# Two transformer blocks on one core: the differential attention's scores in three fp32r passes over high and low parts

## The reference

```python
def diff_attend(q, k, v, lam):
    s = jnp.einsum('bqhmd,bkhmd->bhmqk', q, k).astype(jnp.float32) * (DIFF_QK ** -0.5)
    p = jax.nn.softmax(s, axis=-1)
    a = p[:, :, 0] - lam * p[:, :, 1]
    return jnp.einsum('bhqk,bkhd->bqhd', a.astype(v.dtype), v)
...
    q = apply_rope_2d(group(z, G_DQ).reshape(B, N, HEADS, 2, DIFF_QK), ang_r, ang_c)
    k = apply_rope_2d(group(z, G_DK).reshape(B, N, HEADS, 2, DIFF_QK), ang_r, ang_c)
    v = group(z, G_DV).reshape(B, N, HEADS, HEAD_DIM_2)
    k_all = jnp.concatenate([kc, k], axis=1)
    v_all = jnp.concatenate([vc, v], axis=1)
```

## Time and profile before

| | |
|---|---|
| median of 3 runs | 3357.74 us (3357.29 to 3358.83) |
| the profiled execution | 3358.63 us, span 3357.3 us |
| TensorE busy | 3243.3 us (97%) |
| VectorE busy | 2150.5 us (64%) |
| ScalarE busy | 1389.9 us (41%) |
| mean granted TensorE clock | 0.991 |
| layer 2's attention loop | 1968 to 2113 us |
| layer 3's attention loop | 2814 to 2924 us |

### The profile page before, as it was taken

How to read it: one execution, slowest core, us unless ns; L and a number is a source line. 1 busy time by engine, 2 the same in 40 slices (tenths; PEclk the granted TensorE clock), 3 DMA queues, 4 the chain that set the end, 5 groups by cost and what they waited for, 6 DMA issues and landing times. The chain is left out here.

```text
span 3357.3 us, 45065 instructions
## 1 busy us (share of the span) xinstructions
PE 3243.3 (97%) x17830; PEld 2767.6 (82%) x17830; DVE 2150.5 (64%) x3560; ACT 1389.9 (41%) x2242; POOL 221.0 (7%) x336
## 2 busy tenths in 40 slices
PE   7998999999999999999999999999999999999998
PEld 5787789999978888878878886889999987688887
DVE  5678477888665545558788466476777865654444
ACT  5478353333444324342223345353333444542332
POOL 0001100000000000003111000100000010010001
PEclk9999999999999999999999999999999999999999
DMA  6500124444221221226664211113333231122232
GB/s 242 201 23 1 38 74 128 144 132 140 91 93 46 101 78 47 88 76 200 204 200 167 85 45 51 38 67 116 113 104 110 83 103 57 44 88 94 94 101 76
DMA packets 98689, 334.39 MB, mean 100 GB/s; under 512 B 11872, under 2 KB 16768, under 8 KB 95024
## 3 DMA queue, kind: packets, MB, share of 16 engines
q1 hardware_dynamic: 77072, 252.63, 22.4%
q0 software_dynamic: 21408, 78.88, 7.4%
HBM read 329.37 MB, written 2.10 MB: 99 GB/s over the span
## 5 line engine op out<-in xcount | busy, mean ns | idle before, releaser
L1245 ACT ACTIVATE WH<-WR 128x1024 fp32r<-128x1024 f32 (+3 forms) x516 | 443.1, 863 | 916.0 <-PE PS L638 679.5
L1862 DVE TENSOR_TENSOR WL<-WR,WH 128x1024 fp32r<-128x1024 f32 (+3 forms) x516 | 507.9, 986 | 449.1 <-ACT WH L1245 447.9
L638 PE MATMUL PS<-HH,WH 128*128 128x512 f32 x1608 | 544.2, 373 | 8.7 <-DVE WK L2295 3.4
L638 PE MATMUL PS<-HH,WL 128*128 128x512 f32 x1608 | 539.7, 370 | 0.0
L638 PE MATMUL PS<-HL,WH 128*128 128x512 f32 x1608 | 539.2, 369 | 0.0
L638 PE MATMUL PS<-D,WH 128*128 128x512 f32 x1648 | 420.9, 361 | 1.5 <-DVE D L2319 1.4
L638 PEld LDWEIGHTS PS<-HH,WH 128*128 128x128 f32 x1608 | 280.6, 189 | 69.6 <-issue 9.9
L638 PEld LDWEIGHTS PS<-HL,WH 128*128 128x128 f32 x1608 | 279.4, 189 | 52.8 <-issue 1.0
L638 PEld LDWEIGHTS PS<-HH,WL 128*128 128x128 f32 x1608 | 279.7, 189 | 52.2
L638 PEld LDWEIGHTS PS<-D,WH 128*128 128x128 f32 x1648 | 275.7, 188 | 52.6 <-DVE D L2319 3.2
L638 PE MATMUL PS<-D,WL 128*128 128x512 f32 (+1 forms) x824 | 257.3, 360 | 0.0
(11 more groups left out here) (377 smaller groups left out, 6042.5 us busy)
## 6 DMA issues: line engine op xcount, KB each, us to landing
WR<-in_win SPq DMA_DIRECT2D x176, 512.0 KB, 3.5
AT<-in_adat POOLq DMA_DIRECT2D x144, 512.0 KB, 3.9
WR<-in_wret SPq DMA_DIRECT2D x64, 512.0 KB, 3.7
WR<-in_zin SPq DMA_DIRECT2D x36, 512.0 KB, 3.5
WR<-in_wdn SPq DMA_DIRECT2D x32, 448.0 KB, 3.4
WR<-in_wdn SPq DMA_DIRECT2D x48, 256.0 KB, 2.7
WR<-in_wdn SPq DMA_DIRECT2D x32, 320.0 KB, 3.0
AR<-in_ada SPq DMA_DIRECT2D x8, 1024.0 KB, 19.1
```

The costliest lines, as they stand in the source:

```text
L638: mm = PE.matmul(dst[:, a:b], w(u)[:, k * P:(k + 1) * P], h[:, k, a:b], start=(k == 0 and i == 0), stop=(k == nk - 1 and i == 2))
L1245: AC.activation(M.hi(u), M.raw(u), COPY).then_inc(*on.up("w_hi", u))
L1862: VE.tensor_tensor(M.lo(u), M.raw(u), M.hi(u).bitcast(F32), ALU.subtract).then_inc(*on.up("w_lo", u))
```

## The change

The rotated queries and keys get fp32r copies: QH and KH, the high parts, written by ScalarE in four new copies (`score_high`), and QL and KL, the low parts, written by VectorE in four subtractions at the place of Z's slots 10 and 11 and of DK themselves. ScalarE's four stand around its refills u + 4 + ROWS_AT and u + 5 + ROWS_AT, VectorE's four behind its refill u + 5 + ROWS_AT. The first score waits for the last subtraction, where it waited for the last rotation. Each score is the sum of three matmuls in fp32r (QH x KH, QL x KH, QH x KL), with the two maps' matmuls alternating and the strips as before. The tile NIL shrinks from 768 columns to one that is read broadcast, and CN0, a table of the Fourier mixer, moves behind the new tiles.

```diff
@@ class Memory, mixers @@
+        at = Z + 10 * 4 * T
         self.DK = t("DK", [P, 2, T])
...
-        self.NIL = t("NIL", [P, T])
-        self.top = Z + 96 * 1024
+        self.NIL = t("NIL", [P, 1])
+        self.QH = t("QH", [P, 2, T], F32R)
+        self.KH = t("KH", [P, 2, T], F32R)
         self.CN = [t("CN0", [P, 2, S])]
+        self.top = at
+        self.QL = t("QL", [P, 2, T], F32R)
+        self.KL = t("KL", [P, 2, T], F32R)
@@ tensor_program, mixers @@
                 if j == 0:
-                    PE.wait_ge(*on("roped", (l, 3)))
+                    PE.wait_ge(*on("roped", (l, "low", 3)))
                 w, c0 = nm * P, m0 * P
                 rows = [slice(64 * (h % 2) + 32 * mp, 64 * (h % 2) + 32 * mp + 32) for mp in range(2)]
                 for a in range(0, w, 512):
                     e = min(w, a + 512)
-                    for mp, r in enumerate(rows):
-                        if j and a == 0:
-                            PE.wait_ge(*on("d_max", (l, j - 1, mp)))
-                        mm = PE.matmul(PS[mp][:, a:e], M.Z[r, 10 + h // 2, q * P:(q + 1) * P], M.DK[r, h // 2, c0 + a:c0 + e],
-                                       start=True, stop=True, tile_position=(r.start, 0))
-                        if e == w:
-                            mm.then_inc(*on.up("d_scores", (l, j, mp)))
+                    for i, (qs, ks) in enumerate(((M.QH, M.KH), (M.QL, M.KH), (M.QH, M.KL))):
+                        for mp, r in enumerate(rows):
+                            if j and a == 0 and i == 0:
+                                PE.wait_ge(*on("d_max", (l, j - 1, mp)))
+                            mm = PE.matmul(PS[mp][:, a:e], qs[r, h // 2, q * P:(q + 1) * P], ks[r, h // 2, c0 + a:c0 + e],
+                                           start=i == 0, stop=i == 2, tile_position=(r.start, 0))
+                            if e == w and i == 2:
+                                mm.then_inc(*on.up("d_scores", (l, j, mp)))
@@ scalar_program, mixers @@
-        for v in range(2):
-            refill(u + 4 + ROWS_AT + v)
+
+        def score_high(t):
+            dst, src, w = (M.QH, Z[:, 10 + t, 0:n], n) if t < 2 else (M.KH, M.DK[:, t - 2, :], T)
+            AC.wait_ge(*on("roped", (l, t)))
+            AC.activation(dst[:, t % 2, 0:w], src, COPY).then_inc(*on.up("z_copied", (l, "high", t)))
+
+        score_high(0)
+        refill(u + 4 + ROWS_AT)
+        score_high(1)
+        score_high(2)
+        refill(u + 5 + ROWS_AT)
+        score_high(3)
         AC.wait_ge(*on("product", u + 3 + ROWS_AT))
@@ vector_program, mixers @@
         refill(u + 4 + ROWS_AT)
         rope(3)
         refill(u + 5 + ROWS_AT)
+        for t in range(4):
+            dst, hi, src, w = (M.QL, M.QH, Z[:, 10 + t, 0:n], n) if t < 2 else (M.KL, M.KH, M.DK[:, t - 2, :], T)
+            VE.wait_ge(*on("z_copied", (l, "high", t)))
+            VE.tensor_tensor(dst[:, t % 2, 0:w], src, hi[:, t % 2, 0:w].bitcast(F32), ALU.subtract).then_inc(*on.up("roped", (l, "low", t)))
...
-                    VE.tensor_tensor_reduce(M.dP[mp][j % (3 - mp)][:, 0:w], PS[mp][:, 0:w], M.NIL[:, 0:w], -(32 ** -0.5), 3e38,
+                    VE.tensor_tensor_reduce(M.dP[mp][j % (3 - mp)][:, 0:w], PS[mp][:, 0:w], M.NIL[:, 0:1].to_broadcast([P, w]), -(32 ** -0.5), 3e38,
                                             ALU.add, ALU.min, M.dNM[:, j % 4, mp:mp + 1]).then_inc(*on.up("d_max", (l, j, mp)))
```

## The result

| | before | after |
|---|---|---|
| median of 9 runs | 3357.29 us (3353.09 to 3358.83) | 3367.23 us (3362.30 to 3372.15) |
| ratio to before, 95% interval | | 1.0029 (1.0019 to 1.0039) |
| the profiled execution's span | 3357.3 us | 3366.9 us |

The change makes the kernel 9.9 us, 0.3%, slower; the forecast was 5.8 us. The page after, first its counts: PE has 144 instructions more and 5.6 us less to do, DVE and ACT eight instructions each, and PE's share falls, since it waits more; before stands in the earlier trace rows.

The account below looks back on a forecast made before the run. PE was taken as the bound, with work 97% of the time. Stall + 8.5, clock + 2.7 and gain - 5.4 made + 5.8 us on 3357.74: 3363.5 us, 0.17% slower, range 3355.5 to 3370.0.

Parts of the forecast that it names:

- Burst: Score matmuls of one loop step: 1.25 us with 768 keys, 0.24 less than before; 0.55 with 256 keys, 0.08 less.
- the rival with 3392 us: Score bursts: fp32r matmuls of the two maps do not overlap in strips; + 34.6, 3392.3 us, 1.0% slower; chance 0.13.
- Stall: Start of each loop: first score waits for four subtractions behind the refill; price 4.5 us layer 2, 4.0 layer 3.
- Clock: Behind the two stalls: lowered PE clock costs 2.2 us each, less 1.7 already paid in layer 2; 2.7 us more.
- its own upper bound of 5.0: Clock loss behind the two stalls at most: 5.0 us, with the longer stretch and the cold burst after each.
- Gain: Both loops: shorter bursts on 13 + 8 long steps x 0.24 and 4 short x 0.08, 5.4 us gained.
- Sum: Whole kernel: + 8.5 + 2.7 - 5.4 = + 5.8 us, 3363.5 us, 0.17% slower; forecast case 0.79.
- Nothing of the eight can be hidden there.: Start of layer 2's loop: of the eight new instructions the high copies are early, the four subtractions delay the first score.
- its rival without it (3352.3 us): Loop starts: subtractions are done under the DV product, so no stall; - 5.4 or - 7.2, 3352.3 us; chance 0.03.

Follow-up runs that it names:

- e3: The changed kernel with 22 (layer 2) and 20 (layer 3) unused fp32r matmuls between the DV product and PE's wait for the low parts: 3358.08 us, 1.0004 of before.
- e7: The kernel of e1 with the third score pass (high query x low key) left out: 3346.65 us, 0.9970 of before.
- e6: The kernel before the change with ScalarE's three DV copies put ahead of its refill u + 5 + ROWS_AT: 3362.81 us, 1.0019 of before.
- e1: The changed kernel with the four subtractions and four high copies put ahead of the refill u + 5 + ROWS_AT, where VectorE is idle: 3353.67 us, 0.9988 of before.
- e4: The changed kernel with the score matmuls reordered, all three passes of map 0, then those of map 1: one run, 3363.69 us.

## Why the prediction was right, and where it was off

The time lay in the range and the mechanism was the forecast one: a stall ahead of each loop, half clock behind it, and a gain in the loops that is smaller than the two together. The nearness is not luck by terms that cancel, since the three that missed (clock, gain, late falls of the clock) all missed to the slower side. The interval of the ratio leaves out 1, so the kernel is slower; the prediction was undecided between slower (0.48) and same (0.50), since its 5.8 us lay just under the 6.7 that it held measurable. By its steps:

- **Burst.** Forecast 1.25 and 0.55 us, measured 1.25 and 0.56; a pass of 0.23 per 512 columns (1997.17 to 1997.40) and 0.12 per 256. The strips overlap with fp32r as with fp32; the rival with 3392 us is out, by every burst of the trace. By the Trainium skill's gap of 216 ns for 512 columns ("TensorE: Matmul & The Clock Gate", section "Back-to-back issue gap") the estimate would have been 1.18 us; the trace has 0.23 us per 512 columns in strips too.
- **Stall.** Forecast 6.0 and 5.5 us of standing still and a price of 4.5 + 4.0 = 8.5; measured 5.94 and 5.40, and 4.49 + 3.92 = 8.4 with the clock held (e3). The broadcast read of NIL costs nothing: 0.954 us per maximum against 0.955.
- **Clock: the mis-sized term.** Forecast 2 x 2.2 - 1.7 = 2.7 us. Measured 2.8 + 0.5 + 2.3 = 5.6, less the 1.5 that the kernel before lost, 4.1. (The forecast's 1.7 put six pairs of matmuls at 2.1 us; e7 has 2.27.) To this comes 1.5 us for the late fall in layer 3, which the forecast did not have. The step that failed is taking the mean of what followed two gaps of 3.3 us for gaps of 6 and 5.4: the half clock lasted 7.5 us from the first score on in layer 2, 5.1 in layer 3. The 4.1 lie between the forecast and its own upper bound of 5.0.
- **Gain.** Forecast 5.4. From e3, whose loops have no half clock: layer 2 137.5 (before, less 0.2 us of a slow burst in step 1) - 134.3 = 3.2, where 3.4 were forecast; layer 3 105.8 - 103.4 = 2.4, of which 0.8 is before's own half clock from 2924.2 on (step 15 lasts 17.82 us, 17.06 in e6), so 1.6 of 1.9. Before has another half clock in that loop, from 2893.5 to 2896.9, and this one cost nothing: step 13 is longer by 1.7 us than in e6 (7.23 against 5.55), step 14 shorter by as much (10.67 against 12.32), because PE no longer waits 1.58 us for ACT there. Slow matmuls only took the place of a wait. The forecast overlooked steps 3, 9 and 15 of layer 2: there the shorter burst ends before the Z copy, and they keep 0.08 of 0.24 us. The waits for ACT grew as forecast (0.25 to 0.48 us in layer 3's steps 8 and 10), in step 4 by 0.5, which was not.
- **Sum.** 8.4 + 4.1 - 4.8 + 1.0 for late falls of the clock (1.5 + 0.3 after, 0.8 before) = 8.7, against 8.6 in the table and 9.9 (6 to 13) in the medians. What each late fall cost is read from single traces, and they differ from trace to trace; what brings them is not shown.
- **"Nothing of the eight can be hidden there."** True of the order as written. That the same instructions fit under the DV product (e1) stood in the rows (DVE idle for 4.69 us ahead of the refill); the forecast costed a stall that was one of order, and its rival without it (3352.3 us) is what e1 measures: 3353.7.

## What to carry to other kernels

An operation put ahead of a loop costs what stands between it and its inputs in its engine's program: behind a refill that waits for PE's last product, 3.5 us of VectorE work became 6 us of a standing TensorE; in an idle stretch a few lines earlier it held up nothing, and the first scores followed the DV product by 0.09 us. A stall of TensorE is to be costed with the half clock behind it, here two thirds of the stall's own price again (5.6 on 8.4 us); matmuls that filled the stall took this part away (e3). A faster burst is worth its gain only on steps where nothing else ends last: here 4.8 us arrived of the 7.8 that 30 long and 8 short bursts are shorter, and in e7 about half.

## What the runs showed of the hardware

fp32r matmuls of 32 rows in different strips of the array overlap fully: a pass of both maps takes 0.23 us per 512 columns, as one full-array matmul does, also when the program has three of one strip ahead of three of the other (e4). The Trainium skill ("TensorE: Matmul & The Clock Gate", Part 3, the mechanism of row and column tiling) has matmuls start and end strictly in the order of the program; the trace of e4 does not agree, and the measurement decides. Filling a stall with matmuls whose result nobody reads was worth 8.4 us in the timed runs (e3), 7.3 in the traces, with the first score no earlier.
